# A transformer stack on one core: another opening, with warm-up products, larger transfers and GpSimd rounding four quarter tiles

## The chip, the cores and the metric

The kernel runs on one core of one Trainium2 chip. The metric is the device time of one execution in microseconds. Before the change it is 2240.51 us, the median of three runs (2240.02 to 2240.65).

## The reference

Two different two-layer blocks run one after the other on 256 tokens of width 1024. Only the very beginning matters here: the first layer of the first block begins with a root-mean-square norm and the first product of a gated feed-forward part.

```python
def rms_norm(x, g):
    xf = x.astype(jnp.float32)
    y = xf * lax.rsqrt(jnp.mean(xf * xf, axis=-1, keepdims=True) + NORM_EPS)
    return (y * g.astype(jnp.float32)).astype(x.dtype)

def swiglu_ffn(x, w1, w2):
    a, b = jnp.split(x @ w1, 2, axis=-1)
    return (jax.nn.silu(a) * b) @ w2
```

Everything else (mixers, attention, gates, the second block) follows after it and is untouched. One small constant product also sits in the opening: the relative-position table of the second block, `rel_bias` (32 x 4) against a one-hot matrix (32 x 512), which only the second block needs.

## The kernel before

All weights stand in HBM as one long row of tiles of 128 x 2048 float32 (1 MB). They pass through a ring of five slots (class `Ring`). For each tile SyncE loads `w_raw`, ScalarE writes `w_hi`, a rounded copy in the format that TensorE multiplies fast, and VectorE writes `w_lo = w_raw - w_hi` over the raw tile. The normalised input is kept in the same two parts, transposed, as `hT` (first half of a row: `hT_hi`; second half: `hT_lo`). One product at full accuracy is three of TensorE's: hi by hi, lo by hi, hi by lo (lines 593 to 595).

Every engine has its own written order of work. The order of the opening is class `Start`, with one method for each engine. It treats the first two tiles in quarters ("pieces") of 512 columns, 256 KB each. I count the quarters 0 to 7: 0 to 3 are tile 0, 4 to 7 are tile 1. Quarter c holds the weights of chunk c of the contraction, so the first output, `bank` of token half 0, is made of eight steps c0 to c7 of three products of 512 columns each. Step c needs `w_lo` of quarter c and chunk c of `hT_lo`.

The tokens come in two halves of 128 (t = 0, 1), each a 512 KB load of `x_res`. For each half:

- ScalarE squares both halves of the row and sums them (line 319, two instructions), GpSimd makes the reciprocal root of it (class `Root`: lines 326, 329, 331, the last a power).
- VectorE scales the first 512 columns (`a_xn`, line 374, method `vector_xn`) and ScalarE the other 512 (line 357).
- TensorE transposes `a_xn` in eight products with the identity (line 393), ScalarE writes `hT_hi` (line 365) and VectorE `hT_lo` (line 382, method `vector_lo`), eight instructions each.

The transposes of t = 1 stand on TensorE between c6 and c7 (`Norm.early`). After c7 come the eight steps of token half 1, then tile 2, and so on.

The orders that matter here are these.

- SyncE: x half 0; quarter 0; the two operands of the small product (`a_rel`, `a_onehot`); the identity and the gains (`cols`); quarters 1 to 5; x half 1; quarters 6 and 7; tiles 2, 3 and 4 whole. Then it waits until the small product was copied (`a_line`) and sends it out, loads four constants (1.3 MB), and goes on with tile 5.
- ScalarE: squares of t = 0, `w_hi` 0, scaling, `w_hi` 1, `hT_hi` of t = 0, `w_hi` 2 to 5, squares of t = 1, `w_hi` 6 and 7, scaling, `hT_hi` of t = 1.
- VectorE: scaling, `w_lo` 0 and 1, `hT_lo` of t = 0, `w_lo` 2 to 6, scaling of t = 1, `w_lo` 7, copy of the small product, a reduction of the identity (`four`), `hT_lo` of t = 1, then the whole tiles.
- GpSimd: one fill, then the roots of t = 0 and t = 1.
- TensorE: the small product (line 2613), the transposes of t = 0, c0 to c6, the transposes of t = 1, c7, and so on.

## Time and profile before

| What | Value |
| --- | --- |
| median of the runs | 2240.51 us (2240.02 to 2240.65) |
| profiled execution | 2241.04 us |
| its span in the profile | 2239.3 us |
| TensorE busy | 2222.4 us (99%) |
| VectorE, ScalarE, GpSimd busy | 1530.1, 1209.9, 67.5 us |
| HBM traffic | 182 GB/s over the span |

The profiled execution took 1.7 us more than its span, and 0.5 us more than the median of the runs. The span begins when the first instruction is issued. TensorE's busy time is nearly the whole span, so what remains to be had is the time in which it has nothing to do; a good part of that lies in the opening.

### The profile page before, as it was taken

To read this page: it belongs to the slowest core of one execution; us is meant where nothing else is said; L and a number is where in the kernel's file an instruction comes from. 1 tells how busy PE (TensorE), PEld (TensorE's weight loads), DVE (VectorE), ACT (ScalarE), POOL (GpSimd) and SP (SyncE) were. 2 spreads that over 40 slices of the span, in tenths; PEclk is the share of its full clock that TensorE was granted. 3 is DMA by queue.
4 is the path that set the end of the run, shared out by engine and by line. 5 is a ranking of instruction groups with operands and counts; after the bars stand their busy time and mean duration, and the time that the engine had idled before them with its cause. 6 is when DMAs were issued, how large, how long until landed. Compare 5 with 4: busy or idle time off the path is not lost.

```text
span 2239.3 us, 30453 instructions
## 1 busy us (share of the span) xinstructions
PE 2222.4 (99%) x12350; PEld 1897.7 (85%) x12350; DVE 1530.1 (68%) x2112; ACT 1209.9 (54%) x1812; POOL 67.5 (3%) x118
## 2 busy tenths in 40 slices
PE   8999999999999999999999999999999999999998
PEld 7888987888888889878888888888888988888887
DVE  6557578665665575786656866786777766786766
ACT  6446456454564564555545655455555555455554
POOL 0000000000000000000000200000000100000000
PEclk9999999999999999999999999999999999999999
DMA  8565554455555655544655544445555544445553
GB/s 282 195 234 181 202 179 151 174 187 189 188 184 192 232 184 202 184 146 169 233 188 189 187 151 162 158 152 182 188 193 180 188 151 165 156 164 182 188 188 113
DMA packets 62803, 409.38 MB, mean 183 GB/s; under 512 B 7976, under 2 KB 9512, under 8 KB 15304
## 3 DMA queue, kind: packets, MB, share of 16 engines
q1 hardware_dynamic: 62664, 407.44, 51.0%
q8 instruction: 98, 1.61, 0.3%
q14 instruction: 41, 0.34, 0.0%
HBM read 405.83 MB, written 2.10 MB: 182 GB/s over the span
## 4 chain that ended last, share of the span: by engine, by line
PE 94%; DVE 3%; ACT 1%; DMA 1%; issue 0%; SPq 0%; POOLq 0%; DVEq 0%; POOL 0%; ACTq 0%
PE bank L593 20%; PE bank L594 19%; PE bank L595 19%; PE bank L640 18%; PE bank L647 9%; DVE w_lo L270 1%; PE bank L393 1%; PE bank L1739 1%; PE bank L1751 1%; PE bank L2351 0%; DMA w_raw<-in_tiles 0%; PE bank L2519 0%; PE bank L2058 0%; PE bank L2068 0%; PE bank L2078 0%
## 5 line engine op out<-in xcount | busy, mean ns | idle before, releaser
L270 DVE TENSOR_TENSOR w_lo<-w_raw,w_hi 128x2048 fp32r<-128x2048 f32 x367 | 835.1, 2284 | 56.0 <-ACT w_hi L240 55.2
L240 ACT ACTIVATE w_hi<-w_raw 128x2048 fp32r<-128x2048 f32 x359 | 685.1, 1912 | 109.1 <-DMA w_raw<-in_tiles 108.9
L640 PE MATMUL bank<-hT,w_hi 128*128 128x512 f32 x1920 | 459.5, 390 | 2.3 <-DVE w_lo L270 2.3
L640 PEld LDWEIGHTS bank<-hT,w_hi 128*128 128x128 f32 x1920 | 355.8, 188 | 73.8 <-DVE w_lo L270 2.8
L593 PE MATMUL bank<-w_hi,hT 128*128 128x512 f32 (+2 forms) x832 | 327.7, 394 | 1.6 <-DVE w_lo L223 1.4
L595 PE MATMUL bank<-w_hi,hT 128*128 128x512 f32 (+2 forms) x832 | 318.6, 383 | 0.0
L594 PE MATMUL bank<-w_lo,hT 128*128 128x512 f32 (+2 forms) x832 | 318.3, 383 | 0.0
L647 PEld LDWEIGHTS bank<-hT,w_lo 128*128 128x128 f32 x1920 | 247.7, 191 | 10.3
L647 PE MATMUL bank<-hT,w_lo 128*128 128x256 f32 x1920 | 250.9, 283 | 0.0
L593 PEld LDWEIGHTS bank<-w_hi,hT 128*128 128x128 f32 x832 | 156.6, 188 | 39.3 <-issue 7.9
L595 PEld LDWEIGHTS bank<-w_hi,hT 128*128 128x128 f32 x832 | 156.3, 188 | 31.3
L594 PEld LDWEIGHTS bank<-w_lo,hT 128*128 128x128 f32 x832 | 156.7, 188 | 27.5 <-issue 0.5
L593 PE MATMUL bank<-hT,w_hi 128*128 128x256 f32 x576 | 164.5, 286 | 0.3 <-ACT a_rg L1162 0.3
L595 PE MATMUL bank<-hT,w_lo 128*128 128x256 f32 x576 | 162.9, 283 | 0.0
L594 PE MATMUL bank<-hT,w_hi 128*128 128x256 f32 x576 | 162.9, 283 | 0.0
L896 DVE TENSOR_TENSOR a_ffn_act<-bank,a_ffn_act 128x256 f32<-128x256 f32 x80 | 33.9, 424 | 187.8 <-ACT a_ffn_act L838 187.8
L593 PE MATMUL bank<-w_hi,a_ffn_g_hi 128*128 128x512 f32 x352 | 137.8, 392 | 0.0
L594 PE MATMUL bank<-w_lo,a_ffn_g_hi 128*128 128x512 f32 x352 | 137.4, 390 | 0.0
L595 PE MATMUL bank<-w_hi,a_ffn_g_lo 128*128 128x512 f32 x352 | 137.0, 389 | 0.0
L838 ACT ACTIVATE a_ffn_act<-bank 128x256 f32<-128x256 f32 x80 | 30.5, 381 | 193.4 <-PE bank L647 193.4
L593 PEld LDWEIGHTS bank<-hT,w_hi 128*128 128x128 f32 x576 | 110.4, 192 | 0.9 <-issue 0.7
L594 PEld LDWEIGHTS bank<-hT,w_hi 128*128 128x128 f32 x576 | 110.5, 192 | 0.2
(395 smaller groups left out, 2983.7 us busy)
## 6 DMA issues: line engine op xcount, KB each, us to landing
w_raw<-in_tiles SPq DMA_DIRECT2D x368, 1024.0 KB, 4.8
a_cmp_w<-in_cmp_w SPq DMA_DIRECT2D x2, 2048.0 KB, 7.8
shifted<-in_bias SPq DMA_DIRECT2D x12, 256.0 KB, 7.0
w_raw<-in_tiles SPq DMA_DIRECT2D x8, 256.0 KB, 5.6
a_gm_rows<-in_rows SPq DMA_DIRECT2D x2, 768.0 KB, 7.0
x_res<-in_x SPq DMA_DIRECT2D x2, 512.0 KB, 5.3
a_ret_rows<-in_rows SPq DMA_DIRECT2D x2, 512.0 KB, 8.2
...
```

The lines of the kernel that those rows point to most:

```text
L240: act.activation(k.hi[slot][:], k.raw[slot][:], ACT.Copy).then_inc(k.hi_done[slot], 1)
L270: dve.tensor_tensor(k.lo[slot][:], k.raw[slot][:], k.hi[slot][:].bitcast(F32), ALU.subtract).then_inc(k.lo_done[slot], 1)
L393: last = pe.transpose(self.turned(t, c), self.xn[:, t, c * P:(c + 1) * P], k.ident[:])
L593: pe.matmul(out, w[0], x[0], start=start, stop=False)
L594: pe.matmul(out, w[0], x[1], start=False, stop=False)
L595: return pe.matmul(out, w[1], x[0], start=False, stop=stop)
L640: pe.matmul(bank[:], k.hi[slot][:, w], k.hT[:, c].rearrange("p a s -> p (a s)"), start=c == 0, stop=False)
L647: last = pe.matmul(bank[:, SEQ:2 * SEQ], k.lo[slot][:, w], k.hT_hi[:, c], start=False, stop=c == KC - 1)
L838: act.activation((self.b if half else self.s1)[j][:], self.ab[j][half][:, SEQ:2 * SEQ], ACT.Copy).then_inc(self.copied[j], 1)
L896: dve.tensor_tensor(out[:], self.ab[j][half][:, 0:SEQ], out[:], ALU.add).then_inc(self.summed[j], 1)
L1739: last = pe.transpose(k.bank[2 + u % 2][:, j * P:(j + 1) * P], pr[u % 2][:, j * P:(j + 1) * P], k.ident[:])
L1751: last = pe.matmul(out, self.vsvw[:, kc, d:d + 64], keys, start=False, stop=(br == 1 and kc == 1 and h in (2, 3, 6, 7)))
```

## The change

It touches the opening alone.

- SyncE: quarter 1 goes ahead of the operands of the small product, which now stand behind the identity, the gains and quarter 1. Quarters 2 and 3 become one transfer of 512 KB, and so do 4 and 5, and 6 and 7. The second half of x goes ahead of quarters 4 and 5 (it went behind them). The number of issues ahead of tile 2 falls from 14 to 11.
- GpSimd: fills a part of `hT` with zeros, then the constant; makes the root of t = 0; writes `w_hi` of quarters 2, 3, 4 and 5 (which ScalarE did); then makes the root of t = 1.
- ScalarE: goes from `hT_hi` of t = 0 straight to the squares of t = 1.
- VectorE: scales t = 1 ahead of `w_lo` 6 (it was behind it); the copy of the small product and the reduction go behind `hT_lo` of t = 1.
- TensorE: twelve products of 512 columns on the zeros come first, into a bank that nobody reads; the small product goes behind the transposes of t = 0.
- SyncE's wait for the copied product now uses the semaphore `four_ok`, which a later stage waits for with 2 in place of 1.

```diff
+POOL_PIECES = (2, 3, 4, 5)
+POOL_FILLS = 2
+LANDS = ((0, 1, 2, 2), (0, 0, 2, 2))
+WARM = 12
...
     def piece_load(self, sp, m, q):
         self.loaded = m + 1
-        at = self.places[m]
-        src = self.tiles[at:at + 1, :, q * PIECE:(q + 1) * PIECE]
-        sp.dma_start(self.piece(self.k.raw, m, q), src.rearrange("a p n -> (a p) n")).then_inc(self.k.piece_in[m][q], 16)
+        at, cols = self.places[m], slice(q * PIECE, (q + LANDS[m].count(q)) * PIECE)
+        sp.dma_start(self.k.raw[self.slot[m]][:, cols], self.tiles[at:at + 1, :, cols].rearrange("a p n -> (a p) n")
+                     ).then_inc(self.k.piece_in[m][q], 16)
...
+    def piece_pool(self, pool, m, q):
+        self.piece_landed(pool, m, q)
+        pool.tensor_copy(self.piece(self.k.hi, m, q), self.piece(self.k.raw, m, q)).then_inc(self.k.pool_made, 1)
+
     def piece_lo(self, dve, m, q):
-        dve.wait_ge(self.k.piece_hi, PIECES * m + q + 1)
+        at = PIECES * m + q
+        if at in POOL_PIECES:
+            dve.wait_ge(self.k.pool_made, POOL_FILLS + POOL_PIECES.index(at) + 1)
+        else:
+            dve.wait_ge(self.k.piece_hi, sum(i not in POOL_PIECES for i in range(at + 1)))
...
     def sync(self, sp, line_dram, kept, kept_in):
...
         k.ring.piece_load(sp, 0, 0)
+        sp.dma_start(k.ident[:], w["ident"]).then_inc(self.small_in, 16)
+        sp.dma_start(self.cols1[:], w["cols1"].rearrange("l p n -> p l n")).then_inc(self.small_in, 16)
+        k.ring.piece_load(sp, 0, 1)
         sp.dma_start(self.rel[:], w["rel"]).then_inc(self.rel_in, 16)
         sp.dma_start(self.onehot[:], w["onehot"]).then_inc(self.rel_in, 16)
...
-        for q in range(1, PIECES):
-            k.ring.piece_load(sp, 0, q)
-        for q in range(PIECES):
-            if q == 2:
-                sp.dma_start(k.x[:, 1], x[:, 1]).then_inc(self.x_in[1], 16)
-            k.ring.piece_load(sp, 1, q)
+        k.ring.piece_load(sp, 0, 2)
+        sp.dma_start(k.x[:, 1], x[:, 1]).then_inc(self.x_in[1], 16)
+        k.ring.piece_load(sp, 1, 0)
+        k.ring.piece_load(sp, 1, 2)
         k.ring.loads_to(sp, 5)
-        sp.wait_ge(self.copied, 1)
+        sp.wait_ge(k.four_ok, 1)
...
     def tensor(self, pe):
+        k = self.k
+        pe.wait_ge(k.pool_made, 1)
+        for _ in range(WARM):
+            pe.matmul(k.bank[5][:], k.hT_hi[:, 0, 0:P], k.hT[:, 0].rearrange("p a s -> p (a s)"), start=True, stop=True)
+        pe.wait_ge(self.small_in, 32)
+        self.norm.tensor(pe, 0)
         pe.wait_ge(self.rel_in, 32)
         pe.matmul(self.k.bank[4][0:DIFF_HEADS, :], self.rel[:], self.onehot[:], start=True, stop=True
                   ).then_inc(self.made, 1)
-        pe.wait_ge(self.small_in, 32)
-        self.norm.tensor(pe, 0)
...
     def vector(self, dve):
...
-        for q in range(PIECES - 1):
+        for q in range(2):
             ring.piece_lo(dve, 1, q)
         norm.vector_xn(dve, 1)
-        ring.piece_lo(dve, 1, PIECES - 1)
+        for q in range(2, PIECES):
+            ring.piece_lo(dve, 1, q)
+        norm.vector_lo(dve, 1)
         dve.wait_ge(self.made, 1)
...
-        norm.vector_lo(dve, 1)
...
     def scalar(self, act):
...
         norm.scalar_hi(act, 0)
+        self.root.scalar(act, 1)
         for q in range(2, PIECES):
-            ring.piece_hi(act, 0, q)
-        for q in range(PIECES):
-            if q == 2:
-                self.root.scalar(act, 1)
             ring.piece_hi(act, 1, q)
...
     def pool(self, pool):
-        pool.memset(self.k.neg_half[:], -0.5).then_inc(self.filled, 1)
-        pool.wait_ge(self.filled, 1)
-        for t in range(NT):
-            self.root.pool(pool, t)
+        k = self.k
+        pool.memset(k.hT[:, 0].bitcast(F32), 0.0).then_inc(k.pool_made, 1)
+        pool.memset(k.neg_half[:], -0.5).then_inc(k.pool_made, 1)
+        pool.wait_ge(k.pool_made, POOL_FILLS)
+        self.root.pool(pool, 0)
+        for at in POOL_PIECES:
+            k.ring.piece_pool(pool, at // PIECES, at % PIECES)
+        self.root.pool(pool, 1)
```

The order of instructions on three engines at the opening, first on GpSimd. `x_rstd` is the root of a token half, `w_raw_49` and `w_raw_50` are tiles 0 and 1. Before:

```order
L2656 MEMSET neg_half 128x32
L326 ISA
L326 TENSOR_SCALAR x_rstd<-x_mean_sq 128x1
L329 TENSOR_TENSOR x_rstd<-x_rstd,x_mean_sq 128x1
L331 TENSOR_TENSOR x_rstd<-x_rstd,neg_half 128x1
```

The same three instructions of the root follow once more for t = 1. With the change:

```order
L2674 MEMSET hT 128x512
L2675 MEMSET neg_half 128x32
L342 ISA
L342 TENSOR_SCALAR x_rstd<-x_mean_sq 128x1
L345 TENSOR_TENSOR x_rstd<-x_rstd,x_mean_sq 128x1
L347 TENSOR_TENSOR x_rstd<-x_rstd,neg_half 128x1
L231 CAST w_hi<-w_raw_49 128x512 x2
L231 CAST w_hi<-w_raw_50 128x512 x2
L342 TENSOR_SCALAR x_rstd<-x_mean_sq 128x1
L345 TENSOR_TENSOR x_rstd<-x_rstd,x_mean_sq 128x1
L347 TENSOR_TENSOR x_rstd<-x_rstd,neg_half 128x1
```

Four rounding instructions now stand ahead of the root of t = 1.

On VectorE, from `hT_lo` of t = 0 to the end of the opening, before (`w_lo_54` is tile 0, `w_lo_55` tile 1):

```order
L382 SCALAR_TENSOR_TENSOR hT<-bank,cols,hT 128x128 x8
L223 TENSOR_TENSOR w_lo_54<-w_raw_49,w_hi 128x512 x2
L223 TENSOR_TENSOR w_lo_55<-w_raw_50,w_hi 128x512 x3
L374 TENSOR_SCALAR a_xn<-x_res,x_rstd 128x512
L223 TENSOR_TENSOR w_lo_55<-w_raw_50,w_hi 128x512
L2631 COPY a_line<-bank 4x512
L2632 TENSOR_REDUCE four<-ident 128x32
L382 SCALAR_TENSOR_TENSOR hT<-bank,cols,hT 128x128 x8
```

and with the change:

```order
L398 SCALAR_TENSOR_TENSOR hT<-bank,cols,hT 128x128 x8
L239 TENSOR_TENSOR w_lo_54<-w_raw_49,w_hi 128x512 x2
L239 TENSOR_TENSOR w_lo_55<-w_raw_50,w_hi 128x512 x2
L390 TENSOR_SCALAR a_xn<-x_res,x_rstd 128x512
L239 TENSOR_TENSOR w_lo_55<-w_raw_50,w_hi 128x512 x2
L398 SCALAR_TENSOR_TENSOR hT<-bank,cols,hT 128x128 x8
L2652 COPY a_line<-bank 4x512
L2653 TENSOR_REDUCE four<-ident 128x32
```

`w_lo` of quarter 6 now stands behind the scaling of t = 1, and the copy and the reduction behind `hT_lo` of t = 1.

On SyncE, the loads of the opening, before:

```order
L2583 DMA x_res<-in_x 128x1024
L211 DMA w_raw_49<-in_tiles 128x512
L2585 DMA a_rel<-in_rel 32x4
L2586 DMA a_onehot<-in_onehot 32x512
L2587 DMA ident<-in_ident 128x128
L2588 DMA cols<-in_cols 128x2x24
L211 DMA w_raw_49<-in_tiles 128x512 x3
L211 DMA w_raw_50<-in_tiles 128x512 x2
L2593 DMA x_res<-in_x 128x1024
L211 DMA w_raw_50<-in_tiles 128x512 x2
```

and with the change:

```order
L2599 DMA x_res<-in_x 128x1024
L215 DMA w_raw_49<-in_tiles 128x512
L2601 DMA ident<-in_ident 128x128
L2602 DMA cols<-in_cols 128x2x24
L215 DMA w_raw_49<-in_tiles 128x512
L2604 DMA a_rel<-in_rel 32x4
L2605 DMA a_onehot<-in_onehot 32x512
L215 DMA w_raw_49<-in_tiles 128x1024
L2607 DMA x_res<-in_x 128x1024
L215 DMA w_raw_50<-in_tiles 128x1024 x2
```

The second half of x has moved ahead of everything of tile 1, and six quarter transfers have become three of 128 x 1024.

## Rows read from the trace of the kernel before

**Rows 1.** The page, busy time of each engine.
```profile
PE 2222.4 (99%) x12350; PEld 1897.7 (85%) x12350; DVE 1530.1 (68%) x2112; ACT 1209.9 (54%) x1812; POOL 67.5 (3%) x118
```

**Rows 2.** Waits of TensorE for VectorE, first 60 us: total, times, longest, in us.
```profile
PE bank L593 <- DVE w_lo L223: 1.4, 1, 1.4
```

**Rows 3.** Chain that ended last, opening: start us, us, what.
```profile
5.99 7.36 DMA x_res<-in_x
...
16.00 0.50 PE bank L593
16.50 0.23 PE bank L594
...
17.01 1.10 PE bank L393 x8
...
18.80 0.32 PE bank L593
```

**Rows 4.** Timeline of TensorE, opening.
```profile
7.29 1.97 PE L393 MATMUL bank<-ident,a_xn 128*128 128x128 f32 x8
...
9.84 0.63 PE L594 MATMUL bank<-w_lo,hT 128*128 128x512 f32 x1
```

**Rows 5.** GpSimd's groups by shape, whole run: busy us, mean ns, idle before.
```profile
L331 POOL TENSOR_TENSOR x_rstd<-x_rstd,neg_half 128x1 f32<-128x1 f32 x20 | 11.4, 572 | 1.6
...
L326 POOL TENSOR_SCALAR x_rstd<-x_mean_sq 128x1 f32<-128x1 f32 x20 | 4.5, 224 | 1307.2 <-ACT a_sq L319 558.0 <-ACT b_sq L319 365.4 <-ACT a_sq_m L319 296.3
...
L1555 POOL MEMSET a_cmp_win<- 128x512 f32 x4 | 2.0, 526 | 0.0
...
L1340 POOL TENSOR_SCALAR_AFFINE_SELECT a_gm_wT<-a_gm_wT 128x512 f32<-128x512 f32 x2 | 1.3, 645 | 0.0
...
L2157 POOL COPY b_ml_g<-b_g 128x32 f32<-128x32 f32 x2 | 0.6, 282 | 0.3
...
L163 POOL TENSOR_SCALAR a_ret_rs<-a_ret_mv 128x8 f32<-128x8 f32 x2 | 0.5, 252 | 103.2 <-DVE a_ret_mv L1478 103.2
```

**Rows 6.** Timeline from 29 us: the tile behind the four constants.
```profile
29.56 1.91 ACT L240 ACTIVATE w_hi<-w_raw 128x2048 fp32r<-128x2048 f32 x1 [2.74 <-DMA w_raw<-in_tiles]
...
33.66 0.75 ACT L868 ACTIVATE a_ffn_g_hi<-a_ffn_g 128x256 fp32r<-128x256 f32 x2 [0.22 <-DVE a_ffn_g L917]
...
36.22 0.40 PE L593 MATMUL bank<-w_hi,a_ffn_g_hi 128*128 128x512 f32 x1
```

**Rows 7.** Timeline of VectorE, opening: start us, us, engine, line, operation.
```profile
8.17 0.69 DVE L223 TENSOR_TENSOR w_lo<-w_raw,w_hi 128x512 fp32r<-128x512 f32 x1 [0.65 <-ACT w_hi L218]
...
10.85 2.62 DVE L223 TENSOR_TENSOR w_lo<-w_raw,w_hi 128x512 fp32r<-128x512 f32 x4
...
15.87 0.48 DVE L374 TENSOR_SCALAR a_xn<-x_res,x_rstd 128x512 f32<-128x512 f32 x1
```

**Rows 8.** Issue to landing, us min/median/max: the two halves of x (line 2583, 2593).
```profile
DMA to landing us min/median/max: 3.3/5.3/7.4
```

**Rows 9.** Windows: stretch, busy time of each engine, PEclk, DMA share, GB/s.
```profile
4.00:8.00 4.00, 2.50 (x6) 0.80 (x7) 1.08 (x2) 3.07 (x7) 0.98 (x3) 1.00 0.80 227
...
12.00:16.00 4.00, 2.63 (x12) 1.81 (x10) 2.21 (x5) 3.36 (x9) 0.98 (x3) 1.00 1.02 402
```

**Rows 10.** Issue to landing of quarters 3 and 4, issued at 4.6 and 5.0 us.
```profile
DMA to landing us min/median/max: 4.9/5.6/6.4
```

**Rows 11.** Timeline around 1240 us: GpSimd beside VectorE.
```profile
1240.51 2.28 DVE L270 TENSOR_TENSOR w_lo<-w_raw,w_hi 128x2048 fp32r<-128x2048 f32 x1
1240.72 2.16 POOL L581 TENSOR_SCALAR x_double<-x_double 128x1 f32<-128x1 f32 x1
```

**Rows 12.** Timeline around 200 us: the same two engines, GpSimd first.
```profile
200.81 0.65 POOL L1340 TENSOR_SCALAR_AFFINE_SELECT a_gm_wT<-a_gm_wT 128x512 f32<-128x512 f32 x1
...
200.88 0.85 DVE L374 TENSOR_SCALAR a_xn<-x_res,x_rstd 128x512 f32<-128x512 f32 x1 [0.76 <-POOL x_rstd L331]
```

**Rows 13.** Timeline of GpSimd, opening: the power of t = 1.
```profile
15.12 0.57 POOL L331 TENSOR_TENSOR x_rstd<-x_rstd,neg_half 128x1 f32<-128x1 f32 x1
```

More of the change, by code:

```diff
@@ L154, in __init__ @@
         self.piece_in = [[sem(f"w_piece{m}{q}_in") for q in range(PIECES)] for m in range(SPLIT)]
-        self.piece_hi, self.piece_lo = sem("w_piece_hi"), sem("w_piece_lo")
+        self.piece_hi, self.piece_lo, self.pool_made = sem("w_piece_hi"), sem("w_piece_lo"), sem("pool_made")
         self.res_ok, self.squared, self.rooted, self.xn_dve, self.xn_act, self.turned, self.hT_hi_ok, self.hT_lo_ok = (
@@ L208, in piece_load, with piece_landed @@
         self.loaded = m + 1
-        at = self.places[m]
-        src = self.tiles[at:at + 1, :, q * PIECE:(q + 1) * PIECE]
-        sp.dma_start(self.piece(self.k.raw, m, q), src.rearrange("a p n -> (a p) n")).then_inc(self.k.piece_in[m][q], 16)
+        at, cols = self.places[m], slice(q * PIECE, (q + LANDS[m].count(q)) * PIECE)
+        sp.dma_start(self.k.raw[self.slot[m]][:, cols], self.tiles[at:at + 1, :, cols].rearrange("a p n -> (a p) n")
+                     ).then_inc(self.k.piece_in[m][q], 16)
+    def piece_landed(self, eng, m, q):
+        eng.wait_ge(self.k.piece_in[m][LANDS[m][q]], 16)
     def piece(self, parts, m, q):
@@ L216, in piece_hi @@
     def piece_hi(self, act, m, q):
-        act.wait_ge(self.k.piece_in[m][q], 16)
+        self.piece_landed(act, m, q)
         act.activation(self.piece(self.k.hi, m, q), self.piece(self.k.raw, m, q), ACT.Copy).then_inc(self.k.piece_hi, 1)
         self.hi = m + 1
+    def piece_pool(self, pool, m, q):
+        self.piece_landed(pool, m, q)
+        pool.tensor_copy(self.piece(self.k.hi, m, q), self.piece(self.k.raw, m, q)).then_inc(self.k.pool_made, 1)
     def piece_lo(self, dve, m, q):
-        dve.wait_ge(self.k.piece_hi, PIECES * m + q + 1)
+        at = PIECES * m + q
[3 more added lines that the diff above has]
+            dve.wait_ge(self.k.piece_hi, sum(i not in POOL_PIECES for i in range(at + 1)))
         dve.tensor_tensor(self.piece(self.k.lo, m, q), self.piece(self.k.raw, m, q),
@@ L1657, in tensor @@
         f.tensor(pe, 1)
-        pe.wait_ge(k.four_ok, 1)
+        pe.wait_ge(k.four_ok, 2)
         for i in range(2):
@@ L2576, in __init__ @@
         self.line = r.at("line", 8192, [DIFF_HEADS, self.W])
-        self.small_in, self.rel_in, self.made, self.copied, self.filled, self.line_out = (
-            sem(n) for n in ("small_in", "rel_in", "rel_made", "rel_copied", "filled", "line_out"))
+        self.small_in, self.rel_in, self.made, self.line_out = (
+            sem(n) for n in ("small_in", "rel_in", "rel_made", "line_out"))
     def sync(self, sp, line_dram, kept, kept_in):
@@ L2625, in vector @@
             ring.piece_lo(dve, 0, q)
-        for q in range(PIECES - 1):
+        for q in range(2):
             ring.piece_lo(dve, 1, q)
         norm.vector_xn(dve, 1)
-        ring.piece_lo(dve, 1, PIECES - 1)
+        for q in range(2, PIECES):
+            ring.piece_lo(dve, 1, q)
+        norm.vector_lo(dve, 1)
         dve.wait_ge(self.made, 1)
-        dve.tensor_copy(self.line[:], k.bank[4][0:DIFF_HEADS, :]).then_inc(self.copied, 1)
+        dve.tensor_copy(self.line[:], k.bank[4][0:DIFF_HEADS, :]).then_inc(k.four_ok, 1)
         dve.tensor_reduce(k.four[:], k.ident[:].rearrange("p (q n) -> p n q", q=4), AX.X, ALU.add).then_inc(
             k.four_ok, 1)
-        norm.vector_lo(dve, 1)
         ring.lo_to(dve, 3)
```

2 lines of the change are left out of this document (removed).

## The prediction

> **What bounds the kernel now.** The page's busy times come first [rows 1]: TensorE works 2222.4 us of a span of 2239.3, so the time is the length of its queue, and only its 17 us of idle time can be won. The waits of TensorE put the largest one behind the start at `w_lo`, 1.4 us at line 593 [rows 2]. The chain of waits names its origin [rows 3]. The second half of x, issued at 5.99, lands 7.36 us later at 13.35; ScalarE squares it, makes `w_hi` 6, VectorE makes `w_lo` 6, and step c6 begins at 16.00. From there it is TensorE alone: the transposes of t = 1 at 17.01 (1.10 us), c7, and at 18.80 the first step of token half 1, after which TensorE is never idle for long. So 16.00 and the 2.80 us behind it are the whole question: **a change of the start of c6 is a change of the time**, one for one, unless a later stage takes it back. A single product takes 0.23 us there, a step of three 0.69.
>
> How much could be won at most? c0 to c6 are 21 products, 4.8 us, and start behind the transposes of t = 0 at 7.29 to 9.26 [rows 4]. With all data at hand c6 would begin near 13.5, so no more than some 3 us lie in it, 0.13% of the kernel. What a measurement of this kernel can tell from no change I take as 0.2%, 4.5 us.
>
> **The change part by part.**
>
> *Twelve products on zeros.* They can start once the fill of 128 x 512 is done, 0.53 us [rows 5], at about 1.3. The profile shows the slow clock in the opening: eight transposes take 1.97 us at 7.29 and 1.10 at 17.01 [rows 3, 4], and the product at 9.84 is 0.63 us long where the one at 36.22 is 0.40 [rows 4, 6]. That is the 1.2 GHz level against 2.4. At about twice 0.23 us each the twelve take 5.5 us and end near 6.8, ahead of the transposes. If the clock is up by then, the transposes end 0.9 us earlier and c0, c1 run 1.2 us shorter. None of it reaches c6: c0 waits for `hT_lo`, and c2 for `w_lo` 2, which VectorE begins at 10.85 [rows 7]. Cost and gain: 0.
>
> *The small product* goes behind the transposes of t = 0. At the fast clock it takes about 1 us, between 7.8 and 8.9; c0 could begin at 8.9. If the clock is still low, it takes 1.9 us and c0 begins near 11, c2 near 12.5; c6 at 16 still covers this. Cost: 0.
>
> *The copy and the reduction* (1 us of VectorE) go behind `hT_lo` of t = 1. They stood where VectorE waited for `hT_hi` anyway, so nothing is won. SyncE now waits for the copy until about 21, with the constants and tile 5 queued behind it. By my estimate, eight `hT_lo`, the copy and five issues from 18.1 on, tile 5 is issued near 23.1, some 1.4 us later than before. ScalarE had waited 2.74 us for that tile, until 29.56; its next link to TensorE is `a_ffn_g_hi` at 33.66, 0.4 us long, used at 36.22 [rows 6]. The slack is 2.1 us. Tiles 2 to 4 do not get later, so the lateness stays under 1.4 us. Cost: 0, with little to spare.
>
> *Quarter 1 earlier.* It is issued two places earlier. Before, VectorE waits 0.65 us for `w_hi` 1, until 8.17 [rows 7]; I estimate that half of it goes, so `w_hi` 1, `hT_hi`, `hT_lo` of t = 0 and then `w_lo` 2 move forward by 0.3 us: `w_lo` 2 begins at 10.55, `w_lo` 3 at 11.2, and VectorE is free at 11.85 (2.62 us for four, 0.66 each [rows 7]).
>
> *The loads.* x half 1 gets ahead of two quarters of tile 1. Quarters 4 and 5 now land together at a time L, behind it. The bytes up to and including them are those that stood up to x half 1 before: 2.7 MB. So the upper end of L is 13.35, the landing of x before [rows 3]. For the lower end, x half 0 lands 3.3 us after its issue, at 4.1 [rows 8]; the other 2.25 MB at the 402 GB/s of 12 to 16 us need 5.6 us: 9.7. The truth hangs on how fast larger pieces go in the stretch of 4 to 8 us, where quarters went at 227 GB/s [rows 9]. Quarter 3 took 4.9 us, quarter 4 6.4 [rows 10]. I take the middle, 11.5, since the issue order takes away a part of the early loss and not the queue itself. x half 1 then lands near 10.2, and its squares end well before 12.5 (squares, `w_hi` 6 and `w_lo` 6 together took the 2.65 us up to 16.00 before): **the transfer is no longer what c6 waits for**.
>
> *GpSimd.* No row shows a rounding copy of this size there. Near ones: a select that reads and writes 128 x 512 takes 0.65 us; a copy of 128 x 32 takes 0.28, plus the whole fill of 0.53 gives 0.81 [rows 5]. I take 0.67. The far end comes from the 224 ns of 128 x 1 against the 252 of 128 x 8: 4 ns a column, 2.3 us for 512. Quarters 2 and 3 are rounded from about 9.2 to 10.55, just in time for VectorE.
>
> *GpSimd against VectorE.* The trace shows them block each other. A GpSimd instruction on 128 x 1 takes 224 ns in twenty cases and 2.16 us when VectorE is inside a `w_lo` [rows 5, 11]; it ends with that `w_lo`. The other way round, VectorE's scaling takes 0.85 us beside the 0.65 us select, and 0.48 without [rows 7, 12]: it was held until about 0.44 us after the select began. Now count. GpSimd's rounding of quarter 4 can't read before `w_lo` 3 ends, 11.85 (L = 11.5 is hidden by it), and ends at 12.5; quarter 5 ends at 13.2. `w_lo` 4 wants 12.55 and gets in at 12.95, `w_lo` 5 at 13.6, over at 14.25. The root of t = 1 is three instructions on GpSimd, with a wait between each: the first slips in at the border of the two `w_lo`, the second behind them (14.45), the power takes 0.57: 15.1. Scaling 0.48: 15.6. `w_lo` 6, now behind it, 0.69: 16.3. So **c6 begins at 16.3 instead of 16.0**, and what follows it is as before.
>
> By the Trainium skill ("SBUF — State Buffer", section on the two separate sides) the pair of ports that the two engines share is held for a full instruction. By that rule `w_lo` 4 would get in at 13.2 and c6 begin at 16.5; the 0.85 us of the scaling are shorter than a hold of the full 0.65 us would make them (1.06), so here the rule is too strict.
>
> **The sum.** +0.3 us and nothing else: 2241.04 of the profiled execution becomes 2241.3. The median of the runs is 0.5 us lower, so the forecast is **2240.8 us**, no change that can be told.
>
> **The rivals.**
>
> *A. They hardly block each other.* The power of t = 1 ran from 15.12 to 15.69 [rows 13], and `w_lo` 6, 0.69 us long and done for c6 at 16.00, began inside it without being held; a rounding might hold VectorE as little. Then `w_lo` 4 and 5 follow at 12.5 and 13.2, the root runs beside them from 12.9 to 13.9, scaling ends at 14.4, `w_lo` 6 at 15.1: c6 0.9 us earlier, 2239.6. Against it stands the 2.16 us row.
>
> *B. Transfers or rounding are later.* With L = 13.0 or a rounding of 1 us, quarter 5 is done at 14.4, `w_lo` 5 at 15.3, the root at 16.1, c6 at 17.3: +1.3, 2241.8. For it speaks that the same bytes took until 13.35 before; against it the fewer issues.
>
> The same skill says in "GPSIMD Reference" (section 3.1) that 512 elements take 769 ns at best where the ports do not bind. With 0.77 in place of 0.67 two roundings on the path add 0.2 us, 2241.0.
>
> *C. Slower, beyond what can be told.* GpSimd rounds all four quarters in order ahead of the root, so with a rounding of length r, c6 begins at 9.2 + 4r + 2.2 (root 1.0, scaling and `w_lo` 1.2). It passes 20.5, which is +4.5 us, at r = 2.3. At the far end of the bounds, 2.3 to 2.4 us, this gives 2245.1. Nothing but a row of tiny instructions speaks for such an r.
>
> *D. It does not do what it says.* The clock may rise no sooner, since the products multiply zeros. As worked out, c6 covers that: 2240.8 again.
>
> **How the numbers follow.** Forecast with D 0.43, A 0.28, B 0.27, C 0.02. The range takes A with another half us for early transfers and B with 0.3 more: 2239.1 to 2242.1. Faster by over 0.2% needs 4.5 us, more than the opening holds: 0.01. Slower by over 0.2% is C, 0.02. Within it: 0.97.
>
> **What would show it.** On GpSimd four roundings near 0.67 us, the third beginning with the end of `w_lo` 3, not with its landing; `w_lo` 4 late by about 0.4 us; the first root instruction of t = 1 longer than 0.22; c6 at 16.3 and the first step of token half 1 near 19.1. The first twelve products 0.43 us or so apart and the transposes of t = 0 near 1.1 us. A start of c6 under 15.5 or over 17 makes the sum wrong, a wait of TensorE near 36 us would mean that the slack at tile 5 was misjudged.

## The result, and the profile after

| | before | changed |
| --- | --- | --- |
| median of 22 runs each, us | 2240.43 (2239.87 to 2241.45) | 2242.95 (2241.99 to 2245.11) |
| profiled execution, us | 2241.04 | 2243.23 |
| its span, us | 2239.3 | 2241.5 |
| start of c6 | 16.00 | 17.53 |
| start of token half 1 | 18.80 by the chain, 18.64 by its product's record | 19.91 by the record |
| TensorE's wait near 37 us | 0 | 0.9 |

The ratio is 1.0012, with a 95% interval of 1.0006 to 1.0017: 2.5 us slower, 0.12%. By the 0.2% of the prediction that is no change that can be told, but it lies above the predicted range, whose upper end was 2242.1.

The page's busy times, against [rows 1]:

```profile
PE 2225.7 (99%) x12362; PEld 1900.3 (85%) x12362; DVE 1531.0 (68%) x2112; ACT 1207.9 (54%) x1808; POOL 71.0 (3%) x123
```

TensorE is busy for 3.3 us more. That is not where the time went: the twelve products on zeros, 5.49 us, stand in a stretch where it had nothing to do. What counts is idle time later. The waits of TensorE over the whole run (total, times, longest), against [rows 2]:

```profile
PE bank L609 <- DVE w_lo L239: 2.9, 3, 1.4
...
PE bank L609 <- DVE a_ffn_g_lo L938: 0.9, 1, 0.9
```

There were 1.4 us in one wait for `w_lo`; now 2.9 in three, at c2, c4 and c6. And a wait is new, for `a_ffn_g_lo`. The chain that ended last tells both stories in one piece (start us, us, what), against [rows 3]:

```profile
5.04 8.25 DMA w_raw<-in_tiles
...
13.34 0.15 POOL w_hi L231
...
13.89 0.61 POOL w_hi L231
...
14.60 0.54 POOL x_rstd L342
...
15.21 0.50 POOL x_rstd L345
...
15.78 0.58 POOL x_rstd L347
16.39 0.49 DVE a_xn L390
16.88 0.61 DVE w_lo L239
...
17.53 0.50 PE bank L609
...
21.57 0.58 DVE a_line L2652
...
24.34 9.00 DMA w_raw<-in_tiles
33.37 1.92 ACT w_hi L256
```

Quarters 4 and 5 are issued at 5.04 and land 8.25 us later, at 13.28. GpSimd rounds them, then makes the root; VectorE scales, then makes `w_lo` 6, and c6 begins at 17.53. The chain leaves TensorE there. It goes on over VectorE to the copy `a_line`, over SyncE to tile 5, and over ScalarE's `w_hi` of that tile to the product at 38.49.

The timeline (start us, us, then engine, line and operation), where the steps of the prediction stand:

```profile
1.37 5.49 PE L2630 MATMUL bank<-hT 128*128 128x512 f32 x12 [1.37 <-POOL neg_half L2675]
...
7.71 1.06 PE L409 MATMUL bank<-ident,a_xn 128*128 128x128 f32 x8 [0.85 <-DVE a_xn L390]
...
10.90 1.17 POOL L231 CAST w_hi<-w_raw 128x512 fp32r<-128x512 f32 x2 [3.86 <-DMA w_raw<-in_tiles]
...
11.55 1.67 DVE L239 TENSOR_TENSOR w_lo<-w_raw,w_hi 128x512 fp32r<-128x512 f32 x2 [0.44 <-POOL w_hi L231]
...
12.11 0.63 ACT L335 ACTIVATE a_sq<-x_res 128x512 f32<-128x512 f32 x1 [1.71 <-DMA x_res<-in_x]
...
13.99 1.67 DVE L239 TENSOR_TENSOR w_lo<-w_raw,w_hi 128x512 fp32r<-128x512 f32 x2 [0.77 <-POOL w_hi L231]
```

The transposes of t = 0 take 1.06 us where they took 1.97 [rows 4]: the products on zeros do bring the clock to its 2.4 GHz level. Each pair of `w_lo` takes 1.67 us.

From 20 us on, for the new wait, first the changed kernel's windows (engine busy times, PEclk, DMA share, GB/s), then the same stretch before:

```profile
4.00:8.00 4.00, 3.15 (x10) 2.00 (x9) 0.93 (x2) 2.79 (x7) 0.98 (x3) 1.00 0.84 217
8.00:12.00 4.00, 3.32 (x16) 1.66 (x13) 3.37 (x11) 2.39 (x9) 1.10 (x2) 1.00 0.97 379
12.00:16.00 4.00, 2.55 (x10) 1.80 (x11) 2.88 (x4) 2.40 (x6) 2.49 (x6) 1.00 1.04 424
...
20.00:24.00 4.00, 4.00 (x19) 3.31 (x19) 3.69 (x10) 4.00 (x7) 0.00 (x0) 1.00 0.21 60
```

```profile
20.00:24.00 4.00, 4.00 (x20) 3.27 (x19) 2.81 (x4) 3.75 (x3) 0.00 (x0) 1.00 1.00 374
```

At 20 to 24 us the DMA queue moves 60 GB/s instead of 374: it had run empty. The last part of tile 4 landed at 22.26, and the constants and tile 5 were not issued before the copy. In the opening, 4 to 8 us, the changed kernel moved 217 GB/s, no more than the 227 with quarters [rows 9]. Over all profiles of this document it is 212 to 247 GB/s with the new loads and 227 to 249 with the old ones.

**Where the 2.2 us of the span went.** In both profiles, and in all of the experiments below, the span less the start of token half 1 and less the wait for `a_ffn_g_lo` is 2220.2 to 2221.0 us: before 2239.3 - 18.64 = 2220.7, changed 2241.5 - 19.91 - 0.9 = 2220.7. So the loss is 1.3 us at the start of token half 1 and 0.9 us at that wait.

### The profile page after: what moved, and what is told of

Its sections match the earlier page's. It is cut to its first block, busy times and chain, and to the rows that moved or that the text cites. A ratio compares the mean times of both kernels' runs of the same rounds, so it can differ in the third digit from the quotient of the medians.

```text
span 2241.5 us, 30475 instructions
## 1 busy us (share of the span) xinstructions
PE 2225.7 (99%) x12362; PEld 1900.3 (85%) x12362; DVE 1531.0 (68%) x2112; ACT 1207.9 (54%) x1808; POOL 71.0 (3%) x123
## 4 chain that ended last, share of the span: by engine, by line
PE 94%; DVE 3%; ACT 1%; DMA 1%; issue 0%; SPq 0%; POOL 0%; POOLq 0%; DVEq 0%; ACTq 0%
PE bank L609 20%; PE bank L610 20%; PE bank L611 20%; PE bank L656 17%; PE bank L663 9%; DVE w_lo L286 1%; DMA w_raw<-in_tiles 1%; PE bank L409 1%; PE bank L1755 1%; PE bank L1767 1%; PE bank L2367 0%; PE bank L2074 0%; PE bank L2535 0%; PE bank L2084 0%; PE bank L2094 0%
```

## The experiments

Each kernel was run 11 times, with the kernel before beside it on the same chip (its medians there were 2240.25 to 2240.59). A transfer runs in 16 parts; landings are those of the slowest part, worked out from the DMA records; L is the landing of quarter 5 (before the change x half 1 lands later, at 13.35). "Half 1" is the start of token half 1; "g_lo" the wait near 37 us.

| run | L | c6 | half 1 | g_lo | span | median | ratio, 95% |
| --- | --- | --- | --- | --- | --- | --- | --- |
| before | 12.09 | 16.00 | 18.64 | 0 | 2239.3 | 2240.43 | |
| changed | 13.28 | 17.53 | 19.91 | 0.9 | 2241.5 | 2242.95 | 1.0006 to 1.0017 |
| changed, again | 13.68 | 17.93 | 20.30 | 0.9 | 2241.7 | 2243.45 | 1.0005 to 1.0022 |
| copy back | 12.55 | 17.14 | 19.40 | 0 | 2239.6 | 2241.86 | 0.9999 to 1.0016 |
| ScalarE rounds | 14.02 | 17.09 | 19.47 | 0.3 | 2240.6 | 2241.88 | 0.9998 to 1.0015 |
| loads back | 11.55 | 16.50 | 18.88 | 0.6 | 2240.4 | 2241.89 | 0.9997 to 1.0015 |
| no zero products | 13.88 | 18.13 | 20.50 | 0.6 | 2242.1 | 2243.11 | 1.0002 to 1.0021 |
| scaling back | 14.02 | 17.36 | 20.23 | 0.7 | 2241.5 | 2242.36 | 0.9999 to 1.0017 |
| scaling back, constants first | 13.56 | 16.88 | 19.87 | 0 | 2240.4 | 2241.64 | 0.9997 to 1.0015 |
| loads, scaling, constants | 11.92 | 15.84 | 18.47 | 0 | 2239.4 | 2240.51 | 0.9991 to 1.0009 |

These undo parts of the changed kernel. The next do one part in the kernel before:

| run | c6 | half 1 | g_lo | span | median | ratio, 95% |
| --- | --- | --- | --- | --- | --- | --- |
| copy late | 15.73 | 18.37 | 0.7 | 2239.5 | 2240.98 | 0.9993 to 1.0011 |
| new loads | 17.75 | 20.38 | 0 | 2240.7 | 2242.40 | 1.0000 to 1.0018 |
| new order, still quarters | 16.75 | 19.39 | 0 | 2239.9 | 2241.69 | 0.9997 to 1.0014 |
| zero products | 15.89 | 18.52 | 0 | 2238.8 | 2240.51 | 0.9992 to 1.0009 |
| scaling first | 16.27 | 18.64 | 0 | 2239.3 | 2240.90 | 0.9993 to 1.0011 |
| GpSimd rounds | 16.15 | 18.79 | 0 | 2239.1 | 2240.85 | 0.9992 to 1.0009 |
| copy late, constants first | 16.05 | 18.69 | 0 | 2239.0 | 2240.37 | 0.9990 to 1.0007 |
| quarter 1 and zeros first | 15.61 | 18.25 | 0 | 2239.1 | 2240.71 | 0.9992 to 1.0010 |

The medians move by less than their intervals in most rows. So the reading goes by single waits and starts in the profiles, and by the medians only where they agree.

### The changed kernel again

No edit.

> The changed kernel once more, to see how much the landings of its opening and its time move from execution to execution. Theory 1 (the loss is 1.3 us at c6 and 0.9 us at the wait for tile 5): 2242.9, c6 at 17.5 within 0.3, the 0.9 us wait of TensorE near 38 us is there again. Rival (the profiled execution had a late start of its loads by chance): x half 0 lands by 4.1 instead of 4.7, everything behind it is 0.6 earlier, and c6 begins at 16.9.

c6 is at 17.93, because quarters 4 and 5 landed 0.4 us later still, at 13.68. From L to half 1 it takes 6.62 us here, and 6.63 in the profile above. That number is used below: it takes the luck of the landing out.

### The copy and the reduction back ahead of hT_lo

```diff
+        dve.wait_ge(self.made, 1)
+        dve.tensor_copy(self.line[:], k.bank[4][0:DIFF_HEADS, :]).then_inc(k.four_ok, 1)
+        dve.tensor_reduce(k.four[:], ...)
         norm.vector_lo(dve, 1)
-        dve.wait_ge(self.made, 1)
-        ...
```

> The changed kernel with the copy of the small product and the reduction back ahead of hT_lo of t = 1 on VectorE. Theory 1 (SyncE, held until the copy, lets the DMA queue run empty, and tile 5 lands 3.8 us late): the constants are issued near 18.5 instead of 22.5, tile 5 lands near 30.5 instead of 33.4, the 0.9 us wait of TensorE near 38 us is gone, the start of token half 1 stays at 19.9, and the time is 0.9 us under the changed kernel, 2242.0. Rival (tile 5 is late since the whole DMA queue is late): the wait stays, 2242.9.

Tile 5 lands at 27.4 instead of 33.3, and the wait near 37 us is gone. The span is 1.9 us shorter than the changed kernel's: 0.9 is that wait, 0.5 the earlier start of half 1 (the landing was at 12.55), and 0.5 lies elsewhere, in the band of 2220.2 to 2221.0. But this run shows something else, on its timeline:

```profile
1.36 4.44 PE L2630 MATMUL bank<-hT 128*128 128x512 f32 x12 [1.36 <-POOL neg_half L2675]
...
7.78 1.90 PE L409 MATMUL bank<-ident,a_xn 128*128 128x128 f32 x8 [1.98 <-DVE a_xn L390]
...
11.24 1.28 DVE L239 TENSOR_TENSOR w_lo<-w_raw,w_hi 128x512 fp32r<-128x512 f32 x2
...
12.00 0.63 PE L610 MATMUL bank<-w_lo,hT 128*128 128x512 f32 x1
...
13.25 1.67 DVE L239 TENSOR_TENSOR w_lo<-w_raw,w_hi 128x512 fp32r<-128x512 f32 x2 [0.72 <-POOL w_hi L231]
```

and in its windows (the number before the last two is the granted clock):

```profile
8.00:12.00 4.00, 4.00 (x12) 1.86 (x10) 3.77 (x12) 3.24 (x12) 1.17 (x2) 0.50 1.01 378
12.00:16.00 4.00, 4.00 (x13) 3.16 (x12) 2.54 (x4) 2.16 (x6) 2.77 (x5) 0.67 1.02 423
```

The clock had risen and fell back: after 1.98 us of idle TensorE the transposes take 1.90 us, the products 0.63, and the granted clock is 0.50. TensorE then works without a pause from 7.78 to c6, which begins at 17.14 with its operands ready; half 1 follows L by 6.85 us here instead of 6.63. It is also the run that shows the hold inside itself: a pair of `w_lo` that GpSimd's two roundings just precede takes 1.28 us, the pair beside them 1.67.

### ScalarE rounds quarters 2 to 5 again

```diff
-POOL_PIECES = (2, 3, 4, 5)
+POOL_PIECES = ()
...
+        for q in range(2, PIECES):
+            ring.piece_hi(act, 0, q)
         self.root.scalar(act, 1)
-        for q in range(2, PIECES):
+        for q in range(PIECES):
             ring.piece_hi(act, 1, q)
```

> The changed kernel with ScalarE rounding quarters 2 to 5 again (2 and 3 ahead of the squares of t = 1, 4 and 5 behind them); GpSimd keeps the fills and the roots. Theory 1 (GpSimd's four roundings stand ahead of the root of t = 1, and GpSimd and VectorE block each other): w_lo 4 and 5 take 1.31 us instead of 1.67, the root of t = 1 is ready near 14.8 instead of 16.35, c6 begins at 16.4 instead of 17.5; about 1 us less, 2241.9. Rival (c6 waits for the loads, whoever rounds): c6 within 0.3 of 17.5, 2242.9.

The landing was late, 14.02, and half 1 follows it by 5.45 us instead of 6.63. GpSimd's part in the changed kernel costs 1.2 us behind a landing. Its timeline says why:

```profile
14.60 0.57 POOL L347 TENSOR_TENSOR x_rstd<-x_rstd,neg_half 128x1 f32<-128x1 f32 x1
```

The power of t = 1 is over at 15.17, 1.15 us behind the landing of quarter 5. In the changed kernel it ends at 16.35, 3.07 behind, since the root stands on GpSimd behind the roundings, and so behind the transfer.

### The loads in their old order and sizes

```diff
-LANDS = ((0, 1, 2, 2), (0, 0, 2, 2))
+LANDS = ((0, 1, 2, 3), (0, 1, 2, 3))
...
-        k.ring.piece_load(sp, 0, 2)
-        sp.dma_start(k.x[:, 1], x[:, 1]).then_inc(self.x_in[1], 16)
-        k.ring.piece_load(sp, 1, 0)
-        k.ring.piece_load(sp, 1, 2)
+        for q in range(1, PIECES):
+            k.ring.piece_load(sp, 0, q)
+        for q in range(PIECES):
+            if q == 2:
+                sp.dma_start(k.x[:, 1], x[:, 1]).then_inc(self.x_in[1], 16)
+            k.ring.piece_load(sp, 1, q)
```

> The changed kernel with SyncE's order and the quarter transfers of the kernel before; GpSimd still rounds quarters 2 to 5 ahead of the root of t = 1. Theory 1 (the loads gained nothing; GpSimd's queue is what is late): quarters 4 and 5 are rounded at 11.5 and 12.1, the root runs from 14.2 to 15.7, and w_lo 6, behind the scaling, lets c6 begin at 16.9, 0.6 us less than changed, 2242.3. Rival (the new order of loads costs the most): c6 back at 16.1, 2241.5.

The operands of the small product go back ahead of the identity as well. c6 moves from 17.53 to 16.50. With quarter 5 there at 11.55, it is again x, landed at 12.81, that comes last. The median is 1.1 us below the changed kernel's. The loads are the larger part of the loss at c6, 1.0 of 1.5 us in these two profiles. GpSimd's timeline, and its roundings by their records (ns, shortest, median, longest of four):

```profile
10.33 2.85 POOL L231 CAST w_hi<-w_raw 128x512 fp32r<-128x512 f32 x3 [0.98 <-DMA w_raw<-in_tiles]
13.65 0.75 POOL L342 TENSOR_SCALAR x_rstd<-x_mean_sq 128x1 f32<-128x1 f32 x1 [0.47 <-ACT a_sq L335]
```

```profile
L231 POOL CAST w_hi<-w_raw x4: 609/629/1650, 8.7 to 12.6; 128x512 fp32r<-128x512 f32 x4
```

Of the three roundings in 2.85 us two take 0.61 us. The one between them, from 10.97 on, stands beside two `w_lo` of VectorE (10.86 to 12.15) and takes 1.65. The first instruction of the root takes 0.75, where a free one takes 0.22. The hold works in both directions.

### Without the products on zeros

```diff
-WARM = 12
+WARM = 0
```

> The changed kernel without its twelve products on zeros (the fill stays). Theory 1 (the products reach nothing that c6 waits for): the transposes of t = 0 take 1.9 us and the small product 1.8, c0 begins near 10.9 instead of 9.6, c2 near 12.7; c6 where the landing of quarters 4 and 5 puts it, 4.2 us behind that landing; time that of the changed kernel, 2243.0 to 2243.4. Rival (the fast clock in the opening is worth what was meant): 1 us more, 2244.3. Second rival (the early products cause a fall of the clock in some executions, as in the execution with the copy moved back, where it fell at 7.9 us): fewer long executions, a median 0.3 lower.

The transposes take 1.94 us again and c0 begins at 10.96 instead of 9.64. Half 1 follows the landing by 6.62 us, exactly as with the twelve products. They are worth nothing here, since the later steps wait for their operands either way.

### In the kernel before: the copy late, the loads, the zero products

```diff
+        norm.vector_lo(dve, 1)
         dve.wait_ge(self.made, 1)
         ...
-        norm.vector_lo(dve, 1)
```

> The kernel before with one edit: the copy of the small product and the reduction stand behind hT_lo of t = 1 on VectorE. Theory 1 (SyncE is held until the copy and the DMA queue runs empty, since tiles 2 to 4 have landed by 22.4): the copy is done near 20.9 instead of 17.5, tile 5 is issued near 23 and lands near 32 instead of 29.5, and TensorE waits 0.4 to 0.9 us near 36.5; time 2240.9. Rival (2.1 us of slack cover it, as forecast): tile 5 lands under 31.6, no wait, 2240.3.

Here c6 even begins at 15.73, 0.27 earlier, and the span is still 0.2 longer. TensorE's and ScalarE's timelines:

```profile
31.59 1.92 ACT L240 ACTIVATE w_hi<-w_raw 128x2048 fp32r<-128x2048 f32 x1 [5.09 <-DMA w_raw<-in_tiles]
...
36.71 0.47 PE L593 MATMUL bank<-w_hi,a_ffn_g_hi 128*128 128x512 f32 x1 [0.65 <-DVE a_ffn_g_lo L922]
```

The late copy alone makes the new wait, in a kernel whose loads and rounding are the old ones. Tile 5 is issued 1.1 us later, at 22.80, and lands 2.0 us later, at 31.57. The 2.0 is the least that one can say: the profile before is itself late at this tile, with 29.54, where five kernels with x half 1 in its old place and a filled queue (zero products; copy late, constants first; GpSimd rounds; quarter 1 and zeros first; scaling first) have 27.9 to 28.0.

The new order and sizes of the loads alone, which is the reverse of the diff of the section on the loads, in the kernel before:

> The kernel before with SyncE's new order and transfer sizes alone; ScalarE rounds all quarters in its old order (4 and 5 ahead of the squares of t = 1). Theory 1 (the landings are set by the bytes ahead, so quarters 4 and 5 land at 12.6 to 14.0 instead of 11.4 and 12.1, and x half 1 waits on ScalarE behind them): squares at 14.5, c6 near 17.2, 1.2 us late, 2241.4. Rival (512 KB transfers run faster): quarters 4 and 5 by 12.0, c6 by 15.9, 2240.2.

c6 is at 17.75, and its chain names the reason:

```profile
5.04 9.01 DMA w_raw<-in_tiles
...
14.60 0.61 ACT w_hi L219
15.21 1.23 ACT a_sq L320 x4
16.44 0.53 ACT w_hi L219
...
17.00 0.70 DVE w_lo L224
...
17.75 0.50 PE bank L594
```

Quarters 4 and 5 land at 14.04. ScalarE in its old order rounds them ahead of the squares of x half 1, although x had landed at 12.81. So this run overstates the loads: half 1 is 1.7 us later than before, and in the changed kernel, where the squares do not wait for these quarters, the loads are worth about 1.0. The small product waited for its operands until 7.53 here, ahead of the transposes, and TensorE came to c6 late as well; but the chain does not pass there.

> The kernel before with the fill, the twelve products on zeros first and the small product behind the transposes of t = 0, nothing else. Theory 1 (hidden behind c2 and c6): c6 at 16.0 as before, 2240.3. Rival (the fast clock from 5 to 7 us on moves c0 to c5 and so the end): 2239.7 or less. Rival (the clock falls again in the gap ahead of the transposes, in some executions): a wider spread, a median up to 0.4 higher.

Twelve zero products first and the small product behind the transposes: c0 begins at 9.40, c6 at 15.89 and the median stays at 2240.51. As in the changed kernel, they neither cost nor give.

### The order of the loads, the constants, GpSimd, quarter 1

The new order of the issues with quarters kept apart, in the kernel before:

> The kernel before with SyncE's new order alone but the old quarter transfers (x half 1 ahead of quarter 4; identity, gains and quarter 1 ahead of the small product's operands). Theory 1 (a 512 KB transfer is ready only when the slowest of its parts is, and two quarters let the first half of it be used earlier; the order alone costs less): quarter 3 lands by 10.3 instead of 11.5, x half 1 by 12.6, quarter 4 by 13.0; the first step of token half 1 near 19.4; 2241.3, between before and the 2242.4 of order and size together. Rival (size does nothing, order everything): 20.4 and 2242.4.

c6 at 16.75. Here too ScalarE's squares of t = 1 wait behind the roundings until 14.13, although x had landed at 12.25; quarter 5 landed at 13.57, where quarters 4 and 5 as one came at 14.04. The operands of the small product came at 6.92, which is not on the chain. 13.57 lies inside the 12.55 to 14.04 of the paired transfers, so how much of the late landing is due to the pairing stays open.

In the run with the late copy, the four constants go ahead of the wait:

```diff
         k.ring.loads_to(sp, 5)
+        for dst, src in kept:
+            sp.dma_start(dst, src).then_inc(kept_in, 16)
         sp.wait_ge(self.copied, 1)
         sp.dma_start(line_dram[:, 0], self.line[:]).then_inc(self.line_out, 16)
-        for dst, src in kept:
-            sp.dma_start(dst, src).then_inc(kept_in, 16)
```

> The kernel before with the copy and the reduction behind hT_lo of t = 1, as in the run with that edit alone, but SyncE issues the four constants ahead of its wait for the copy. Theory 1 (it is the empty DMA queue that makes tile 5 late): the constants land by 26, tile 5, issued near 21.7, lands before 29.5, and the 0.7 us wait of TensorE near 37 is gone; 2240.3. Rival (VectorE's later copy and reduction delay w_lo of tiles 2 and 3): the wait stays, 2241.0.

Its windows and ScalarE's timeline:

```profile
20.00:24.00 4.00, 4.00 (x20) 3.30 (x19) 3.69 (x6) 3.80 (x3) 0.00 (x0) 1.00 1.03 403
```

```profile
27.90 1.92 ACT L240 ACTIVATE w_hi<-w_raw 128x2048 fp32r<-128x2048 f32 x1 [1.07 <-DMA w_raw<-in_tiles]
```

The queue stays full, tile 5 is ready 3.7 us earlier than with the late copy alone, and the wait is gone. So it was the empty queue and not the copy's 0.67 us.

GpSimd's four roundings and ScalarE's earlier squares in an otherwise old opening:

> The kernel before with one part of the change: GpSimd rounds quarters 2 to 5 ahead of its root of t = 1 and ScalarE does not (it still fills the zeros); loads, orders of VectorE and TensorE as before. Theory 1 (the roundings cost where they land late and stand in front of the root and of w_lo 6; here they end near 13): a rounding takes 0.61 us, w_lo pairs beside it over 1.5 us instead of 1.3, x half 1 is still what c6 waits for; c6 at 15.9 to 16.1, 2240.6. Rival (GpSimd's part costs by itself): the root of t = 1 later than 15.7, c6 over 16.4, 2241.2 or more.

```profile
8.15 1.70 POOL L231 CAST w_hi<-w_raw 128x512 fp32r<-128x512 f32 x2 [1.62 <-DMA w_raw<-in_tiles]
...
11.63 1.54 POOL L231 CAST w_hi<-w_raw 128x512 fp32r<-128x512 f32 x2 [1.77 <-DMA w_raw<-in_tiles]
```

With x as the last transfer, the roundings are done at 13.17 before its squares, and the root is not behind them. c6 at 16.15 follows the landing of x (13.49) by 2.66 us, as before the change (2.65). GpSimd's rounding costs nothing where its transfer does not come last.

Zero products, quarter 1 ahead of the small operands, and the constants first, in the kernel before:

> The parts of the change that cost nothing, on the kernel before: products on zeros first, small product behind the transposes of t = 0, quarter 1 ahead of its operands, and the constants ahead of SyncE's wait for the copy; all transfers in quarters, x half 1 where it was. Theory 1 (x half 1 lands when the bytes ahead of it are through, 13.1 to 13.4): c6 at 15.8 to 16.0, 2240.4, level with the kernel before. Rival (quarter 1 earlier pulls c6 along): 2240.0 or less.

c6 at 15.61 and half 1 at 18.25, the earliest of all, and yet the median, 2240.71, is not below the 2240.47 of the kernel before beside it: a wait of TensorE for `a_rg` (line 1162), 0.3 us before, is 0.5 here. What the opening gives is taken back in part by a later stage, and the rest is below what these runs can tell.

### VectorE's scaling and w_lo 6

The 4.2 us from L to c6 have one more part, the order on VectorE. Scaling back behind `w_lo` 6, in the changed kernel:

```diff
-        for q in range(2):
+        for q in range(PIECES - 1):
             ring.piece_lo(dve, 1, q)
         norm.vector_xn(dve, 1)
-        for q in range(2, PIECES):
-            ring.piece_lo(dve, 1, q)
+        ring.piece_lo(dve, 1, PIECES - 1)
```

> The changed kernel with w_lo 6 again ahead of VectorE's scaling of t = 1, nothing else. Theory: with the scaling first, VectorE idles 0.74 us in the changed kernel for the root (16.39) while w_hi 6 lies ready, and w_lo 6 pays for it. Back in its place, w_lo 6 follows w_lo 5 directly: the landing L of quarters 4 and 5 plus 2.4 is the end of w_lo 5, plus 0.7 is the start of c6: 16.4 at L = 13.3, 16.8 at 13.7, so c6 starts 3.1 us behind the landing instead of 4.25. The power of the root may be held by w_lo 6 and the scaling then begins near 16.9, so the start of token half 1 gains only about 0.6: 19.3 to 19.7. Tile 5 is earlier by as much, its wait stays near 0.9. Median 2242.0 to 2242.5. Rival: the order of the two costs nothing, since the root is the chain either way: c6 still 4.2 behind the landing, median 2243.0.

c6 now follows L by 3.34 us instead of 4.25, but half 1 by 6.21 instead of 6.63, a gain of 0.4. The power, which took 0.57 us, is held by `w_lo` 6, and TensorE then waits before the transposes instead, for `w_lo` 7 behind the scaling:

```profile
16.52 0.91 POOL L347 TENSOR_TENSOR x_rstd<-x_rstd,neg_half 128x1 f32<-128x1 f32 x1
```

```profile
18.60 1.09 PE L409 MATMUL bank<-ident,a_xn 128*128 128x128 f32 x8 [0.40 <-DVE w_lo L239]
```

That, and the constants ahead of the wait:

> r12 and also the four constants issued ahead of SyncE's wait for the copied product. Theory: the queue no longer runs empty behind tile 4, tile 5 is then bound by its slot and issued near 22.4, lands by 29, ScalarE's w_hi of it by 29, so TensorE's wait near 37 us (0.9) is gone altogether. Median 0.9 below r12: 2241.1 to 2241.6. Rival: the wait comes from the late start and not from the constants: it stays at 0.6 or more, median as r12.

The wait near 37 us is 0 and the queue moves 361 GB/s at 20 to 24 us. The median is 0.7 us below the run before. In the changed kernel too, the constants are the cause. Half 1 follows L by 6.31 us, a gain of 0.3.

The same two lines swapped in the kernel before:

> The kernel before with the scaling of t = 1 ahead of w_lo 6, nothing else. Theory (the order is a cost of its own, which my sum did not price): w_lo 6 could begin at 15.26 and now waits for the end of the power, 15.7, and the scaling, 0.4 to 0.5: 16.15, so c6 starts at 16.9 instead of 16.0 (3.5 us behind the landing of x instead of 2.65). The transposes of t = 1 have their input earlier but stand behind c6: token half 1 starts 0.8 later, median 2241.2. Rival: costs nothing: c6 near 16.0, median 2240.5.

c6 follows x (12.74) by 3.53 us instead of 2.65, as expected, yet half 1 by 5.90 instead of 5.29 (18.64 - 13.35): c7's operand is there at once. The swap costs 0.6 us where x comes last. That is clear of the scatter: in the seven profiles with x last and the old order on VectorE, with GpSimd's roundings, zero products or the late copy among them, half 1 follows x by 5.29 to 5.31 us. With the loads back and the swap still in, it was 6.07.

The three together, loads back, scaling back, constants first, in the changed kernel:

> The changed kernel with three things back or added: the old order and sizes of the loads, w_lo 6 ahead of the scaling, and the four constants ahead of SyncE's wait. Left of the change: zero products, GpSimd's four roundings, the late small product and copy. Theory: the three are the whole loss, so c6 starts 2.7 us behind the landing of x half 1, 15.5 to 16.1, token half 1 at 18.2 to 18.7, no wait near 37 us: median 2240.1 to 2240.7, level with the kernel before. Rival: GpSimd's rounding has its own price through the hold on VectorE and on the root: c6 0.4 later than that, median 2241.0 or more.

c6 at 15.84, no wait near 37 us, a median of 2240.51 beside 2240.51: the loss is gone. What is left of the change (zero products, GpSimd's four roundings, late product and copy) costs and gives nothing. No version was faster than the kernel before by more than its interval.

## Why the prediction was wrong

**The opening as the bound, right.** A start of token half 1 that is later by 1.3 us shows one for one in the span. The start of c6 does not quite: from c6 to half 1 it is 2.38 us in the changed kernel and 2.64 before, where the transposes had waited for `w_lo` 7 (16.26 to 16.95). So 1.5 us at c6 became 1.3. The size of what could be won or lost there was right too; no variant left the band of 2240.4 to 2243.5.

**The landing L, wrong, 1.8 us.** It was taken as 11.5, the middle between 9.7 and 13.35. It was 13.28, and 12.55 to 14.04 in the other runs with these loads. The lower end was worked out at 402 GB/s, as if the early stretch could go at the speed of the later one. It did not: the changed kernel moved 217 GB/s at 4 to 8 us. But the 1.8 us do not lie there. What the queues had moved by 11.5 us, before and with the change:

```profile
DMA packets 1669, 2.76 MB, mean 240 GB/s; under 512 B 472, under 2 KB 600, under 8 KB 1669
```

```profile
DMA packets 1386, 2.84 MB, mean 247 GB/s; under 512 B 442, under 2 KB 570, under 8 KB 1386
```

As many bytes as the prediction counted, 2.7 MB, were through by 11.5 us in both kernels, so 11.5 was a fair value for the bytes as a whole. What the sum left out is that a transfer is there with its last part. In the changed kernel the middle part of quarters 4 and 5 (the median of the 16) came at 11.57 and the last at 13.28. In all eight profiles with these loads the middle part came at 11.2 to 11.6, and the last at 12.55 to 14.04. Before, it was 11.79 and 13.35 for x half 1: the 13.35 held that spread already, and the value to take was this upper end. The forecast had the order of the issues take away a part of the early loss. This was rival B. The prediction's own sign for a wrong sum, a start of c6 over 17, came. Behind x (12.08) the transfer was still the last one, so "no longer what c6 waits for" was wrong.

**From L to c6, right in its sum.** The prediction counted 4.8 us from 11.5 to 16.3, of which 0.35 were the wait for `w_lo` 3; from a late L it gave 4.3 (rival B: 13.0 to 17.3). Measured are 4.25. A rounding took 0.61 us (0.67 taken), the hold of VectorE 0.39 per pair (0.4 for `w_lo` 4), the first two instructions of the root 0.53 and 0.49 (more than 0.22 expected).

"SBUF — State Buffer" of the Trainium skill, in the section on the two separate sides, has the port pair held for the full instruction. A rounding that begins at 13.89 would then hold `w_lo` 4, ready at 13.99, until 14.50, 0.51 us; the pair is 0.39 longer. The rule is nearer than the 0.44 of 0.65 us in [rows 12] made it, but still a little too strict. The Trainium skill's "GPSIMD Engine Reference" (section 3.1) has 769 ns for 512 elements as the best case of a tight loop; the row has 0.61 us for this rounding, so the measurement decides.

**GpSimd in the order, half seen.** The count had the root behind the roundings, but priced it at L = 11.5, where nothing waits for it. The price by itself, 1.2 us against ScalarE's rounding, comes only with a late L; the forecast had that combination in rival B alone, which it gave 0.27. The scaling ahead of `w_lo` 6 was put into the count without a price; it is 0.3 to 0.4 us in the changed kernel, 0.6 in the old one.

**The copy, wrong, 0.9 us.** "Cost: 0, with little to spare" rested on three figures. Tile 5 was issued at 24.34 and not near 23.1, 1.2 us later since the whole opening was. Its lateness at landing was 3.8 us, not "under 1.4": 2.65 at the issue, and more since the queue had run empty and the constants had to start it again. The slack was not 2.1 but 1.5 us: the last link before TensorE is not `a_ffn_g_hi` at 33.66 but VectorE's `a_ffn_g_lo`. It begins at 34.11 before and at 37.92 now, and the product can begin 0.57 us behind that (38.49), so before it could have begun at 34.68 instead of 36.22:

```profile
34.11 0.76 DVE L922 TENSOR_TENSOR a_ffn_g_lo<-a_ffn_g,a_ffn_g_hi 128x256 fp32r<-128x256 f32 x2 [0.16 <-ACT a_ffn_g_hi L868]
```

```profile
37.92 0.76 DVE L938 TENSOR_TENSOR a_ffn_g_lo<-a_ffn_g,a_ffn_g_hi 128x256 fp32r<-128x256 f32 x2 [0.15 <-ACT a_ffn_g_hi L884]
...
38.49 0.47 PE L609 MATMUL bank<-w_hi,a_ffn_g_hi 128*128 128x512 f32 x1 [0.88 <-DVE a_ffn_g_lo L938]
```

3.8 less the 1.3 by which TensorE itself is later, less 1.5 of slack, is 1.0, and 0.9 was measured. Both the 3.8 and the 1.5 are measured from a profile whose tile 5 was late (29.54). From the 27.9 of the five other kernels the lateness is 5.4 and the slack 3.1; the difference is the same. The prediction named this wait as the sign that the slack was misjudged, and the sign came.

**The zero products and the small product, right:** twelve in 5.49 us (5.5 taken), the transposes 1.06 us long, and neither gains nor costs (6.62 us from L to half 1 with and without them).

**Rivals.** B had 2241.8 with c6 at 17.3; the c6 was right to 0.2 us, and most of the rest of the 2242.95, 0.9 us, is the tile that no rival priced. A, few blocks, falls with the pairs of 1.28 and 1.67 us. C falls with the rounding at 0.61, D with the transposes.
